# The output projection of attention, the norm before the MLP and the MLP in one block of programs

## The reference

```python
y = o @ w_out                                   # fox_mixer's last line
x = x + g_m * y                                 # g_m: a row of D gates
h = rms_norm_2(x, norm_mlp[i]) * (1 + sc_f) + sh_f
x = x + g_f * (jnp.square(jax.nn.relu(h @ w_mlp_in[i])) @ w_mlp_out[i])
```

## Time and profile before

| | |
|---|---|
| median of three runs | 2783.83 us |
| profiled execution, own time | 2777.85 us |
| its span, first to last instruction | 2776.1 us |
| TensorE busy | 2434.8 us (88% of the span) |
| VectorE busy | 1866.8 us (67%) |
| ScalarE busy | 1231.7 us (44%) |
| mean granted TensorE clock | 0.939 of full speed |
| results of the output projection end on TensorE | about 2024.9 us from the start |
| first matmul of the MLP | 2072.79 us from the start |

### The profile page before, as it was taken

The page is one execution under the profiler, slowest core; times in us unless marked ns, Lnnn a source line. Parts: engine busy times, 40 slices in busy tenths (PEclk is TensorE's granted clock), DMA queues, the critical chain, the costliest instruction groups (busy, mean ns, idle before and its releaser), DMA issues. The chain is left out here.

```text
span 2776.1 us, 34024 instructions
## 1 busy us (share of the span) xinstructions
PE 2434.8 (88%) x12070; PEld 2049.3 (74%) x12070; DVE 1866.8 (67%) x2415; ACT 1231.7 (44%) x1758; POOL 364.4 (13%) x365
## 2 busy tenths in 40 slices
PE   3888889599999999941489999996959999999999
PEld 2666678478887888841389999995848888888887
DVE  5878367588888888857257888886454554545545
ACT  2242323277777777743156766765132112121111
POOL 1006644111111110024111111110010000000000
PEclk8999999699999999975699999997969999999999
DMA  6677365599687999975111111112321111111111
GB/s 235 189 243 258 118 214 204 200 354 400 240 315 287 386 401 395 398 271 191 51 31 47 47 47 54 47 35 77 129 81 41 60 45 45 45 45 60 45 46 61
DMA packets 135799, 446.88 MB, mean 161 GB/s; under 512 B 14350, under 2 KB 73330, under 8 KB 122392
## 3 DMA queue, kind: packets, MB, share of 16 engines
q1 hardware_dynamic: 118476, 382.10, 37.8%
q10 hardware_dynamic: 9596, 35.75, 3.2%
q0 software_dynamic: 7632, 27.79, 2.8%
HBM read 388.84 MB, written 56.76 MB: 161 GB/s over the span
## 5 line engine op out<-in xcount | busy, mean ns | idle before, releaser
L1637 PE MATMUL psum<-w_high,block_hT_high 128*128 128x512 f32 x576 | 233.5, 405 | 20.7 <-DVE w_low L1248 18.0
L2543 DVE TENSOR_TENSOR x<-x,psum 128x512 f32<-128x512 f32 x256 | 173.0, 686 | 112.3 <-PE psum L1639 112.3
L1639 PE MATMUL psum<-w_high,block_hT_low 128*128 128x512 f32 x576 | 226.7, 394 | 0.0
L1638 PE MATMUL psum<-w_low,block_hT_high 128*128 128x512 f32 x576 | 226.5, 393 | 0.0
L1248 DVE TENSOR_TENSOR w_low<-w_up,w_high 128x2048 fp32r<-128x2048 f32 x72 | 161.8, 2289 | 87.7 <-ACT w_high L1242 87.7
L1637 PE MATMUL psum<-w_qkv_high,fox_hT_high 128*128 128x384 f32 x512 | 181.7, 355 | 34.5 <-DVE w_qkv_low L2177 27.4
L1637 PE MATMUL psum<-hT_high,w_mlp_in_high 128*128 128x512 f32 x512 | 200.2, 391 | 7.1 <-DVE w_mlp_in_low L2520 7.1
L1639 PE MATMUL psum<-hT_high,w_mlp_in_low 128*128 128x512 f32 x512 | 199.9, 390 | 0.0
L1638 PE MATMUL psum<-hT_low,w_mlp_in_high 128*128 128x512 f32 x512 | 199.9, 390 | 0.0
L1637 PE MATMUL psum<-w_mlp_out_high,hiddenT_high 128*128 128x512 f32 x512 | 199.2, 389 | 0.0
L1638 PE MATMUL psum<-w_mlp_out_low,hiddenT_high 128*128 128x512 f32 x512 | 199.2, 389 | 0.0
(11 more groups left out here) (404 smaller groups left out, 6195.1 us busy)
## 6 DMA issues: line engine op xcount, KB each, us to landing
w_gate<-in_w_expert_gate SPq DMA_DIRECT2D x32, 2048.0 KB
w_up<-in_w_expert_up SPq DMA_DIRECT2D x32, 2048.0 KB, 9.3
w_down<-in_w_expert_down SPq DMA_DIRECT2D x32, 2048.0 KB, 10.9
v_aug<-in_w_ada SPq DMA_DIRECT2D x48, 512.0 KB, 4.5
expert_rows<-block_out ACTq DMA_DIRECT2D x36, 512.0 KB, 9.7
v_aug<-in_ada_w SPq DMA_DIRECT2D x32, 512.0 KB, 4.7
expert_rows<-w_in_low ACTq DMA_DIRECT2D x8, 2048.0 KB, 8.3
w_mlp_in<-in_w_mlp_in SPq DMA_DIRECT2D x16, 1024.0 KB, 5.0
```

What stands on the lines that cost most here:

```text
L1637: pe.matmul(out, sh, mh, start=start, stop=False)
L1638: pe.matmul(out, sh, ml, start=False, stop=False)
L1639: return pe.matmul(out, sl, mh, start=False, stop=stop)
L2543: dve.tensor_tensor(x3[:, t, at], x3[:, t, at], bank[4 + j % 4], ALU.add).then_inc(s_r, 1)
```

## The change

The three blocks become one, `fox_out_mlp`. The norm of tile t is begun when both halves of its rows have been added, and TensorE transposes the tiles between the remaining results of the projection. `hT_high` and `hT_low` hold the attention outputs first and are overwritten tile by tile (128 token columns over all 8 k) once both results of the tile are made. Buffers are shared: the raw slices of `o` lie in `n_xn`, those of `w_out` in the MLP's first weight buffer `w_mlp_in`, the scale row in the squares' buffer `n_sq`; the MLP's split weights lie where `w_out`'s were. The last 8 results use banks 0 to 3 in turn, the transposes banks 4 to 7. The four rows (gate, gain, scale, shift) are loaded behind slice 2 of the weights; x and then the MLP's first `w_mlp_in` piece come behind the last slice, `w_mlp_out` and its gate row after the last result of the projection. The transposes of tile 7, the last, stand between the second and the third group of the MLP's first step. Nothing that is computed changes.

```diff
         phase(attention, x2_dram, f_dram, heads_dram, free=False)
         with ExitStack() as xs:
             x3 = sbuf(xs, "x3", [P, TT, D])
-            phase(fox_out, x2_dram, heads_dram, x3, free=False)
             hTh = sbuf(xs, "hT_high", [P, KT, S], F32R)
             hTl = sbuf(xs, "hT_low", [P, KT, S], F32R)
-            phase(mlp, x3, hTh, hTl, out)
+            phase(fox_out_mlp, x2_dram, heads_dram, x3, hTh, hTl, out)
...
-def fox_out(nc, a, sbuf, sem, psum, bank, ident, ones, mhalf, mods, x2_dram, o_dram, x3):
-
-    with ExitStack() as c2:
...
-def mlp(nc, a, sbuf, sem, psum, bank, ident, ones, mhalf, mods, x3, hTh, hTl, out):
+def fox_out_mlp(nc, a, sbuf, sem, psum, bank, ident, ones, mhalf, mods, x2_dram, o_dram, x3, hTh, hTl, out):
...
+        stat = sbuf(c2, "n_stat", [P, TT, 2])
+        with ExitStack() as early:
+            wh = sbuf(early, "fox_w_out_high", [P, KT, D], F32R)
+            wl = sbuf(early, "fox_w_out_low", [P, KT, D], F32R)
+            xn = sbuf(early, "n_xn", [P, 2, D])
+            mix = sbuf(early, "fox_mix", [P, 2, HALF])
+            grow = sbuf(early, "fox_gate_row", [P, D])
+            gain = sbuf(early, "n_gain", [P, D])
+            shift = sbuf(early, "n_shift", [P, D])
+            sq = sbuf(early, "n_sq", [P, D])
         w2 = sbuf(c2, "w_mlp_out", [P, 2, D])
-        grow = sbuf(c2, "mlp_gate_row", [P, D])
-        l1, l2, s_gr = sem("h_w1"), sem("h_w2"), sem("h_gate_row")
-        w1_d = a["w_mlp_in_2"][0].rearrange("(p k) n -> p k n", k=KT)
-        w2_d = a["w_mlp_out_2"][0].rearrange("(f p) n -> p f n", p=P)
-
-        def first_weights(sp):
-            sp.dma_start(w1[:], w1_d[:, :, 0:W]).then_inc(l1, 16)
-            sp.dma_start(w2[:], w2_d[:, 0:2, :]).then_inc(l2, 16)
-            sp.dma_start(grow[:], mods[6 + GATE_F:7 + GATE_F, :].to_broadcast([P, D])).then_inc(s_gr, 16)
-
-        with ExitStack() as c3:
-            norm_turn(nc, c3, "n", sbuf, sem, psum, ident, mhalf, a["norm_mlp_2"], mods, 6 + SCALE_F, 6 + SHIFT_F, hTh, hTl, x3, None, first_weights)
+        frow = sbuf(c2, "mlp_gate_row", [P, D])
...
+        wraw = w1[:].rearrange("p k n -> p (k n)").rearrange("p (u n) -> p u n", u=2)
+        oraw = xn
...
+        def turned(t):
+
+            return psum[:, 4 + 2 * (t % 2):6 + 2 * (t % 2), :].rearrange("p b (k t) -> p (b k) t", t=P)
...
+                for k in range(KT):
+                    if k >= 2:
+                        sp.wait_ge(s_lo, 2 * (k - 1))
+                    sp.dma_start(oraw[:, k % 2, :], o_d[:, k, :]).then_inc(s_lo_[k % 2], 16)
+                    sp.dma_start(wraw[:, k % 2, :], w_d[:, k, :]).then_inc(s_lw_[k % 2], 16)
+                    if k == 2:
+                        sp.dma_start(grow[:], mods[6 + GATE_A:7 + GATE_A, :].to_broadcast([P, D])).then_inc(s_row, 16)
+                        sp.dma_start(gain[:], a["norm_mlp_2"].to_broadcast([P, D])).then_inc(s_row, 16)
+                        sp.dma_start(sq[:], mods[6 + SCALE_F:7 + SCALE_F, :].to_broadcast([P, D])).then_inc(s_row, 16)
+                        sp.dma_start(shift[:], mods[6 + SHIFT_F:7 + SHIFT_F, :].to_broadcast([P, D])).then_inc(s_row, 16)
+                sp.dma_start(x3[:], x2_dram.rearrange("(t p) n -> p t n", p=P)).then_inc(s_x, 16)
+                sp.wait_ge(s_lo, 2 * KT)
+                sp.dma_start(w1[:], w1_d[:, :, 0:W]).then_inc(l1, 16)
+                sp.wait_ge(s_m, NO)
+                sp.dma_start(w2[:], w2_d[:, 0:2, :]).then_inc(l2, 16)
+                sp.dma_start(frow[:], mods[6 + GATE_F:7 + GATE_F, :].to_broadcast([P, D])).then_inc(s_gr, 16)
...
+            @block.gpsimd
+            def _(pool):
+                for t in range(TT):
+                    pool.wait_ge(n_sq, t + 1)
+                    pool.tensor_scalar(stat[:, t, 0:1], stat[:, t, 0:1], 1.0 / D, EPS, ALU.mult, ALU.add).then_inc(n_e, 1)
+                    pool.wait_ge(n_e, t + 1)
+                    pool.tensor_tensor(stat[:, t, 1:2], stat[:, t, 0:1], mhalf[:], ALU.pow).then_inc(n_rs, 1)
...
+                def mixed(j, b, k):
+                    t, hf = divmod(j, 2)
+                    rows, at = slice(t * P, (t + 1) * P), slice(hf * HALF, (hf + 1) * HALF)
+                    return split_mm(pe, bank[b], (hTh[:, k, rows], hTl[:, k, rows]), (wh[:, k, at], wl[:, k, at]), k == 0, k == KT - 1)
+
+                def turn_rows(t):
+                    pe.wait_ge(n_sh, t + 1)
+                    if t >= 2:
+                        pe.wait_ge(n_lo, t - 1)
+                    for k in range(KT):
+                        ins = pe.transpose(turned(t)[:, k, :], xn[:, t % 2, k:D:KT], ident[:])
+                    ins.then_inc(n_tr, 1)
+
+                for k in range(KT):
+                    pe.wait_ge(s_lo, 2 * k + 2)
+                    for j in range(TT):
+                        ins = mixed(j, j, k)
+                        if k == KT - 1:
+                            ins.then_inc(s_m, 1)
+                for j in range(TT, NO):
+                    pe.wait_ge(s_g, j - TT + 1 if j < TT + 4 else j - 3)
+                    for k in range(KT):
+                        ins = mixed(j, (j - TT) % 4, k)
+                    ins.then_inc(s_m, 1)
+                    if j == TT + 2:
+                        turn_rows(0)
+                        turn_rows(1)
+                    if j == TT + 4:
+                        turn_rows(2)
+                        turn_rows(3)
+                    if j == TT + 5:
+                        turn_rows(4)
+                    if j == TT + 6:
+                        turn_rows(5)
+                turn_rows(6)
+
                 def products(n, u, last):
+                    first = isinstance(n, int) and n == 0
...
+                        if first:
+                            pe.wait_ge(n_lo, 4 + 4 * hf)
+                            if hf == 0:
+                                pe.wait_ge(s_g, NO - 3 + g)
...
+                        if first and g == 1:
+                            turn_rows(TT - 1)
...
-                over_blocks(pe, products)
+                products(0, 0, False)
+                products(1, 1, False)
+                with pe.Fori(1, NB // 2 - 1) as i:
+                    for u in range(2):
+                        products(i * 2 + u, u, False)
+                for u in range(2):
+                    products(NB - 2 + u, u, u == 1)
...
+                def square(t):
+                    act.wait_ge(s_res, 2 * t + 2)
+                    if t >= 1:
+                        act.wait_ge(n_sq, t)
+                    act.activation(sq[:], x3[:, t, :], ACT.Square, accum_out=stat[:, t, 0:1]).then_inc(n_sq, 1)
+
+                def high_rows(t):
+                    act.wait_ge(n_tr, t + 1)
+                    act.wait_ge(s_m, 2 * t + 2)
+                    act.activation(hTh[:, :, t * P:(t + 1) * P], turned(t), ACT.Copy).then_inc(n_hi, 1)
...
+                act.wait_ge(n_gain, 1)
+                square(0)
+                square(1)
+                square(2)
+                square(3)
+                high_rows(0)
+                high_rows(1)
+                square(4)
+                high_rows(2)
+                high_rows(3)
+                square(5)
+                high_rows(4)
+                square(6)
+                high_rows(5)
+                act.wait_ge(s_m, NO)
                 high1(0, 0)
+                high_rows(6)
+                square(7)
+                high_rows(7)
...
+                def add_mix(t):
+                    for hf in range(2):
+                        j = 2 * t + hf
+                        at = slice(hf * HALF, (hf + 1) * HALF)
+                        dve.wait_ge(s_m, j + 1)
+                        if j >= 2:
+                            dve.wait_ge(s_res, j - 1)
+                        dve.tensor_tensor(mix[:, j % 2, :], bank[j if j < TT else (j - TT) % 4], grow[:, at], ALU.mult).then_inc(s_g, 1)
+                        dve.wait_ge(s_g, j + 1)
+                        dve.tensor_tensor(x3[:, t, at], x3[:, t, at], mix[:, j % 2, :], ALU.add).then_inc(s_res, 1)
+
+                def scaled_rows(t):
+                    dve.wait_ge(n_rs, t + 1)
+                    if t >= 2:
+                        dve.wait_ge(n_tr, t - 1)
+                    dve.scalar_tensor_tensor(xn[:, t % 2, :], x3[:, t, :], stat[:, t, 1:2], gain[:], ALU.mult, ALU.mult).then_inc(n_sc, 1)
+                    dve.wait_ge(n_sc, t + 1)
+                    dve.tensor_tensor(xn[:, t % 2, :], xn[:, t % 2, :], shift[:], ALU.add).then_inc(n_sh, 1)
+
+                def low_rows(t):
+                    dve.wait_ge(n_hi, t + 1)
+                    dve.tensor_tensor(hTl[:, :, t * P:(t + 1) * P], turned(t), hTh[:, :, t * P:(t + 1) * P].bitcast(F32), ALU.subtract).then_inc(n_lo, 1)
...
+                dve.wait_ge(s_row, 64)
+                dve.scalar_tensor_tensor(gain[:], sq[:], 1.0, gain[:], ALU.add, ALU.mult).then_inc(n_gain, 1)
+                dve.wait_ge(n_gain, 1)
```

(63 more changed lines are left out.)

57 lines of the change are left out of this document (removed).

## The result

| | before | change |
|---|---|---|
| median | 2784.35 us (4 runs, 2782.35 to 2789.26) | 2761.85 us (4 runs, 2761.45 to 2766.35) |
| profiled execution, own time and span | 2777.85, 2776.1 us | 2762.02, 2760.3 us |
| mean granted clock | 0.939 | 0.943 |

The ratio is 0.992, with a 95% interval of 0.9903 to 0.9937: 22.5 us faster, where 34.1 were forecast. 2761.85 lies 1.85 us above the range.

What follows compares the result with a forecast made beforehand. Bound: a 47.9 us TensorE hole between projection and MLP. Group 4's end moves from 2096.8 to 2035.8 + 10.9 + 1.7 + 1.06 + 2.3 + 10.9 = 2062.7; gain 34.1, 2783.8 - 34.1 = 2749.7, say 2750; range 2743 to 2760.

Steps and rivals of the forecast that it cites:

- Behind the mark the work is the same.: After the end of the MLP's group 4, work is unchanged; that mark moves from 2096.8 to 2062.7, gain 34.1 us.
- the second wait: TensorE waits 2.3 us for tile 7's last low part, between MLP groups 2 and 3; clock loss 0, bound 1.7.
- The first matmul of the MLP: It starts at 2035.8 instead of 2072.79, once DVE has made the weights' low part.
- the thin margins at tiles 4 and 6: DVE scales these tiles 0.6 and 0.7 us before TensorE asks for them among the projection's last results.
- the rows ahead of slice 3 and x: Four spread rows loaded first delay slice 3 by 0, at worst 3 us, and x by 0, bound 1.
- The clock: Half speed behind the gap before the MLP costs 0 to 2.2 us; 1.7 taken, from a gap in attention.
- the first wait: TensorE idles 3.2 us before the MLP's first matmul, until the weights' low part is made.
- rival B: More stalls: margins at two tiles tip, second gap drops the clock, slice 3 late; gain 25 to 31, chance 0.22.
- C: Less is lost: no clock drop at the first gap either; gain 36 us, 2748; chance 0.12.
- E: No gain: the norm's steps wait on each other, each of eight tiles 4 us late; chance 0.03.
- D: Slower: interleaved transposes keep TensorE at the lower clock until the end of group 4; 2806 us, chance 0.03.
- The rule of the Trainium skill: Transposes do not count as busy for the clock, so both gaps would drop it; 2751 to 2752 us.

Runs made afterwards that it cites:

- e3: The kernel before with 64 unused bytes behind w_mlp_in, nothing else: median 2796.33 us against 2784.82, ratio 1.0041.
- e5: The change with n_stat enlarged to 2048 bytes a partition, so operands stand a multiple of 2048 bytes apart: median 2746.95 us, ratio 0.9856.
- e6: e5 with tile 7's transposes behind the first group of the MLP's first step instead of the second: median 2747.59 us, ratio 0.9857.
- e1: The change with n_stat twice as large, 128 bytes a partition instead of 64: median 2763.39 us, ratio 0.9925.
- e2: As e1, with 64 more bytes ahead of hT_high: median 2766.56 us, ratio 0.9933.

## Why the prediction was right, and where it failed

**The step that failed** is "Behind the mark the work is the same." The work was, its price was not: 684.26 us against 674.34, for 64 bytes between the two operands of the MLP's first products. I had followed every instruction and transfer through the new buffers, but not their addresses. The forecast had no term and no rival for it. By the traces, the forecast 34.1 us and the measured 22.1 differ by 12.0: 9.9 are this, 2.2 lie between the first MLP matmul and the first output product (1.7 for the clock behind the second wait, some 0.5 for pitch), and 0.2 came back before them. e3 shows the cause in the old program, e5 takes it out of the new one. With it out, the gain by the trace is 34.1 us, the forecast's number, and the median 2746.95 lies 3 us under the 2750 forecast. Part of that exactness is luck: two things were off and cancelled, as below.

**The first matmul of the MLP.** Forecast 2072.79 - 2035.8 = 37.0 us earlier, measured 37.2. TensorE waits 3.44 us there (forecast 3.2). The order step by step held: transposes ready at every tile, the thin margins at tiles 4 and 6 not tipped, eight transposes in 1.05 us (1.06), DVE's first read 42.2 us behind the projection's first matmul (41.8 before), so the rows ahead of slice 3 and x cost nothing that can be seen.

**The second wait.** 2.37 us, forecast 2.3.

**The clock.** Behind the first wait it is 0.62 and 0.52 in two windows, and matmuls 0.43 us apart cost 1.7 us, as taken. The working for this 1.7 was off: in attention TensorE's matmul came at 1425.61 and the clock was back at 1428.5, so by those rows 2.9 us of work ran at half speed and 1.4 were lost. For the second wait I took 0 with 1.7 as the bound; the windows show 0.89, 0.50 and 0.76, so it is the bound. That part of rival B happened; B's other two parts did not. e6 has neither the second wait nor the drop. But the wait alone does not decide it: e1 and e2 have the same two waits (3.44 and 2.37 us) and the same order, and there the clock stays at 1.00 behind the second one, while it is low for longer behind the first (in each of them 12 matmuls of 0.43 us stand there, against 7 in the change). Windows of e1, the first four from its first MLP matmul at 2044.18 on, the last two from its matmul behind the second wait, at 2061.57:

```profile
2044.00:2046.00 2.00, 1.82 (x4) 1.49 (x5) 2.00 (x3) 0.00 (x0) 0.71 (x2) 0.50 0.78 311
2046.00:2048.00 2.00, 2.00 (x6) 1.56 (x5) 1.68 (x2) 0.00 (x0) 0.00 (x0) 0.50 1.03 363
2048.00:2050.00 2.00, 2.00 (x6) 1.51 (x6) 0.00 (x0) 0.00 (x0) 0.00 (x0) 0.50 0.39 137
2050.00:2052.00 2.00, 2.00 (x10) 1.65 (x9) 0.00 (x0) 0.00 (x0) 0.00 (x0) 0.97 0.00 0
...
2062.00:2064.00 2.00, 2.00 (x11) 1.61 (x10) 1.71 (x1) 0.17 (x1) 0.00 (x0) 1.00 0.00 0
2064.00:2066.00 2.00, 2.00 (x10) 1.65 (x9) 0.22 (x1) 2.00 (x2) 0.00 (x0) 1.00 0.00 0
```

Both ways cost nearly the same in sum: from the first MLP matmul to the first output product e1 takes 28.65 us, e5 28.69 and the change 29.12. What decides between them is open.

From the first MLP matmul to the first output product the forecast has 26.9 us; measured are 29.1, of which 1.7 are this drop and some 0.5 the pitch. In e5 it is 28.7, and there the first matmul came 2.0 us before the forecast (98.84 against 2035.8 - 1934.99 = 100.8), which cancelled the drop. The first matmul is 1.7 us earlier in e5 than in the change: 0.7 are the projection's pitch over its 384 matmuls (0.2289 in the change; 0.2267 and 0.2273 in e5), and 1.0 is the shorter low clock at the projection's start, which is luck of that execution as far as the runs tell.

**Rivals.** C (no drop at the first wait) and E are out. D is out: the clock stays at 1.00 from 1977 to 2042, through 56 transposes in five places. The rule of the Trainium skill that was weighed there ("TensorE: Matmul & The Clock Gate", "Part 4: PE-mode transpose") gave 2751 to 2752, with a drop at both waits; both came in the change, in e5 too, but in e1 and e2 only the first. And no run shows that a drop came because transposes went ahead of the wait: none has a wait of this length without them.

## What to carry to other kernels

Where buffers are freed in another place, allocation is part of the change: print the addresses of the operands of the dominant matmuls before and after, and keep the distance of moving and stationary operand a multiple of 256 bytes, which was the fast case in every run here (0.2267 us for these products). When TensorE is full in both traces and the time differs, count the matmuls in the same stretch, or take the distance of their starts, before looking for waits. A hole that depends on one late tile is worth a second look at the order: in e6 one line moved removed a wait and, in that execution, a stay at half clock, 4 us by the trace.
